# First mixer reordered by direction, its head outputs and gate rows moved beside other work, and weight splitting moved from GpSimd to ScalarE and VectorE

## The chip, the cores and the metric
The kernel runs on one core of a Trainium2 chip. The metric is device time in microseconds of one execution; three runs before the change took 2997.96, 3000.23 and 3006.75 us (median 3000.23).

## What is computed
Two transformer layers on 512 tokens of width 1024 (three kinds of attention, then a gated feed-forward network each), then one block with two recurrent mixers over 256 context and 512 latent tokens, then a last feed-forward network and norm. The change lies in the recurrent block. In fp32, cut to what matters:

```python
u, u_c = modulate(rms_norm(x)), modulate(rms_norm(ctx))      # latent and context tokens
p = split_cols(u @ w_in)      # first mixer: q, k, v, gate, low rank; second: q, k, v, gate; 16 gate rows; branches
# first mixer (gated linear attention), 4 heads of 128 keys x 256 values, both directions
log_a = log_sigmoid(low_rank @ w_up + b_dec) / 16            # one decay per token and key
b = cumsum(log_a within a chunk of 64)
scores = mask((q * exp(b)) @ (k * exp(-b)).T)
o = scores @ v + (q * exp(b)) @ S ;  S = exp(b_last) * S + (k * exp(b_last - b)).T @ v
y_gla = rms_norm(o, per head) * silu(gate)
# second mixer (mLSTM), 4 heads on the tokens in column order, both directions
f = log_sigmoid(gate rows f), i = gate rows i                # 4 rows x 4 heads of 768 tokens
m = running max of (m + f, i); rows of weights from f, i, m; convolution and silu on q and k
h = scan with those weights;  y_m = rms_norm(h) * sigmoid(gate)
x = x + g1 * ((sigmoid(b0) * (y_gla @ w0) + sigmoid(b1) * (y_m @ w1)) @ w_out)
```

## The kernel before, in words
Each engine has a program of its own, written out by hand as one Python function per engine; they meet at semaphores only, and each engine takes its queue in order. A `Program` counts what it has waited for; a `Banks` ring hands out PSUM banks: `fill` on TensorE waits until the bank's last content has been read, `take` on the reader waits until it is full. In this block ScalarE reads the ring `ab` (three banks: projections, transposed keys, decay inputs) and VectorE the ring `db` (two banks: scores, states, outputs). The `job`s of one ring must be taken in the order in which TensorE fills them.

*Projections.* A product of fp32 accuracy is three matmuls on high and low parts (`parts_steps`, 8 steps of 3 matmuls). The weights of the two mixers come as 24 pieces of 1 MB (`SECOND`: for each head `qk`, `v`, `gate`), loaded by SP alternately into two places (`PLACE`): piece j is loaded when piece j - 2 has been read for the last time. GpSimd waits for each landing and makes the high part (a cast) and the low part (a subtraction), `split_piece` (L762); TensorE waits for `piece_split`. GpSimd also brings the first four of eight tiles of the tokens into column order (`permute`, L597; VectorE does the other four) once all heads of the first mixer have been projected, and after that goes on with the pieces of the second mixer, the branches and the output.

*First mixer.* For each head, TensorE issues: decay inputs of direction 0, q of the next head, decay inputs of direction 1, k and two of the six v tiles of the next head, then `gla_scan` (L1263) for direction 0 and for direction 1, the rest of the next head's projections between them, then gate 1 and `head_outputs` (L1294: eight transposes). A scan is: scores, six key transposes, eleven state products (some projection steps between them), four outputs. ScalarE makes the decays (`decay_exponents`, L1868): two evacuations with the bias, abs, exp, ln, then, when VectorE has made the chunk sums, three exponents and one more. VectorE (`decays`, L2307) makes min, subtraction, scan, differences, and the decayed q, k (two forms). The tiles W1 to W5 are shared by both directions, so one direction's decays follow the other's. Then VectorE masks the scores, updates the states, adds the outputs (`gla_outputs`, L2338) and in `head_outputs` (L2350) scales by the root that ScalarE's `head_norm` (L1892) gives.

*Gate rows.* After the fourth head: 16 gate rows are projected, picked apart by four small products into 4 heads x 4 rows (`GR`), ScalarE adds the bias and makes abs, exp, ln; then `rows` (L2388) on VectorE for both directions, with q and k of the second mixer's first two heads on TensorE beside them. The second mixer starts when both directions are done.

The lines that set the order of one head on TensorE before:

```python
                decay_inputs(h, 0)
                if h + 1 < NH2:
                    run(nxt("q"))
                decay_inputs(h, 1)
                ...
                gla_scan(h, 0, nxt)
                gla_scan(h, 1, nxt)
                run(nxt("gate", 1))
                head_outputs()
```

## Time and profile before
| | |
|---|---|
| profiled execution | 3005.11 us, span 3003.2 us |
| TensorE busy | 2759.6 us, 92% |
| VectorE / ScalarE / GpSimd busy | 1296.2 / 986.0 / 1001.6 us |
| mean granted clock of TensorE | 0.951 of full speed |
| chain that ended last | PE 73%, DVE 9%, ACT 8%, DMA 6%, issue 2% |

In the profile PE is TensorE's matmuls and PEld its weight loads, DVE is VectorE, ACT ScalarE, POOL GpSimd, SP the engine that issues loads. Stretches are given in microseconds from the start of the span. PEclk is the granted clock of TensorE as a share of 2.4 GHz. A busy TensorE at half clock does half the work, so busy time alone doesn't tell how much of a stretch could go.

### The profile page before, as it was taken

How to read it: one execution, taken by the hardware profiler on the slowest of the kernel's cores; microseconds unless marked ns; L12 is line 12 of the kernel's file. 1: busy time of each engine (PE TensorE's matmuls, PEld its weight loads, DVE VectorE, ACT ScalarE, POOL GpSimd, SP SyncE). 2: the span in 40 equal slices, each digit the busy share in tenths (PEclk: the TensorE clock that was granted, in tenths of full speed). 3: DMA queues.
4: the chain of work that ended last, by engine and by line, in shares of the span. 5: the costliest groups of instructions: out<-in, count | busy, mean ns of one | idle time of the engine just before them, and what ended most of it. 6: DMA issues, size and time to landing. Idle time of an engine off the chain costs nothing.

```text
span 3003.2 us, 35461 instructions
## 1 busy us (share of the span) xinstructions
PE 2759.6 (92%) x13958; PEld 2141.7 (71%) x13958; DVE 1296.2 (43%) x1755; ACT 986.0 (33%) x1652; POOL 1001.6 (33%) x683
## 2 busy tenths in 40 slices
PE   7988999999999799999998888596998999899997
PEld 6866658887797574888876666465876565688886
DVE  2758445443354863544333344526333212333322
ACT  5468422222344872222223344322222100222221
POOL 5565403436545660134562322411220223200000
PEclk9999999999999999999998999797998999899998
DMA  5230024554422002355452111011111331233322
GB/s 127 91 65 1 19 70 119 148 134 133 140 75 84 18 1 59 104 137 139 133 145 66 43 29 42 28 29 28 43 43 42 80 88 57 65 104 95 88 87 67
DMA packets 386053, 230.39 MB, mean 77 GB/s; under 512 B 9340, under 2 KB 382204, under 8 KB 385888
## 3 DMA queue, kind: packets, MB, share of 16 engines
q1 hardware_dynamic: 383408, 224.09, 27.1%
q0 software_dynamic: 1952, 1.94, 0.8%
q8 instruction: 111, 1.82, 0.3%
q10 hardware_dynamic: 528, 2.10, 0.2%
q14 instruction: 54, 0.44, 0.0%
HBM read 226.01 MB, written 2.10 MB: 76 GB/s over the span
## 4 chain that ended last, share of the span: by engine, by line
PE 73%; DVE 9%; ACT 8%; DMA 6%; issue 2%; POOL 0%; SPq 0%; DVEq 0%; ACTq 0%; POOLq 0%
PE ps L815 63%; PE scores L815 7%; DMA raws<-in_w_down 5%; PE ps L957 1%; ACT wH L1770 1%; DVE R L2058 1%; DVE R L2316 1%; ACT R L1895 0%; DVE spare L2068 0%; ACT U L1609 0%; DMA ring<-in_w_in 0%; DVE R L2314 0%; DVE QK_parts L2048 0%; ACT spare L1632 0%; DVE R L2356 0%
## 5 line engine op out<-in xcount | busy, mean ns | idle before, releaser
L815 PE MATMUL ps<-xH,wH 128*128 128x512 f32 x1000 | 396.9, 397 | 8.3 <-DVE xL L2227 8.3
L815 PE MATMUL ps<-xL,wH 128*128 128x512 f32 x1000 | 391.3, 391 | 0.0
L815 PE MATMUL ps<-xH,wL 128*128 128x512 f32 x1000 | 390.9, 391 | 0.0
L1770 ACT ACTIVATE wH<-raws 128x2048 fp32r<-128x2048 f32 (+1 forms) x114 | 192.9, 1692 | 503.8 <-PE ps L815 307.3
L2253 DVE TENSOR_TENSOR wL<-raws,wH 128x2048 fp32r<-128x2048 f32 (+1 forms) x113 | 233.7, 2068 | 286.4 <-ACT wH L1770 286.3
L815 PE MATMUL ps<-ring_parts,U_parts 128*128 128x256 f32 (+1 forms) x1936 | 311.7, 290 | 12.8 <-DVE ring_parts L2110 6.2
L716 POOL TENSOR_TENSOR spare<-spare,cvec 128x1024 f32<-128x1024 f32 x64 | 124.5, 1946 | 563.6 <-DMA spare<-in_w_ada 563.6
L815 PE MATMUL ps<-R 128*64 128x128 f32 (+6 forms) x1768 | 276.6, 344 | 29.3 <-DVE R L2334 4.6
L815 PEld LDWEIGHTS ps<-ring_parts,U_parts 128*128 128x128 f32 x1936 | 277.7, 197 | 25.9 <-issue 22.6
L815 PEld LDWEIGHTS ps<-R 128*64 128x64 f32 (+2 forms) x1768 | 171.3, 166 | 131.1 <-issue 77.0
L768 POOL CAST ring_parts<-ring 128x2048 fp32r<-128x2048 f32 x28 | 54.6, 1951 | 547.5 <-DMA ring<-in_w_in 540.5
L815 PE MATMUL ps<-U_parts,ring_parts 128*128 128x512 f32 (+2 forms) x720 | 217.1, 392 | 18.3 <-ACT R L1863 18.3
L815 PEld LDWEIGHTS ps<-xH,wH 128*128 128x128 f32 x1000 | 188.7, 189 | 52.9 <-issue 8.5
L815 PE MATMUL ps<-R,ring 128*128 128x512 f32 x496 | 217.5, 596 | 1.3 <-DVEq L56 1.3
L815 PEld LDWEIGHTS ps<-xH,wL 128*128 128x128 f32 x1000 | 188.9, 189 | 39.8
L815 PEld LDWEIGHTS ps<-xL,wH 128*128 128x128 f32 x1000 | 189.0, 189 | 38.4 <-issue 1.0
L815 PE MATMUL ps<-hH,wH 128*128 128x512 f32 x528 | 210.6, 399 | 1.1 <-DVE wL L2253 1.1
L815 PE MATMUL ps<-hL,wH 128*128 128x512 f32 x528 | 207.5, 393 | 0.0
L815 PE MATMUL ps<-hH,wL 128*128 128x512 f32 x528 | 207.0, 392 | 0.0
L718 POOL TENSOR_TENSOR spare<-spare 128x512 f32<-128x512 f32 (+2 forms) x192 | 199.4, 1038 | 15.1
L815 PEld LDWEIGHTS ps<-R,ring 128*128 128x128 f32 x496 | 94.4, 191 | 113.9 <-issue 111.2
L815 PEld LDWEIGHTS ps<-U_parts,ring_parts 128*128 128x128 f32 (+1 forms) x720 | 134.1, 192 | 56.5 <-issue 28.2
(408 smaller groups left out, 4697.5 us busy)
## 6 DMA issues: line engine op xcount, KB each, us to landing
raws<-in_w_gate_up SPq DMA_DIRECT2D x88, 512.0 KB, 5.5
ring<-in_w_in SPq DMA_DIRECT2D x34, 1024.0 KB, 5.9
spare<-in_w_ada SPq DMA_DIRECT2D x64, 512.0 KB, 4.1
raws<-in_w_down SPq DMA_DIRECT2D x32, 704.0 KB, 6.1
raws<-in_w_ffn_in SPq DMA_DIRECT2D x44, 512.0 KB, 5.1
ring<-in_w_in SPq DMA_DIRECT2D x22, 512.0 KB, 6.0
raws<-in_w_ffn_out SPq DMA_DIRECT2D x16, 704.0 KB, 4.5
ring<-in_w_o SPq DMA_DIRECT2D x6, 896.0 KB, 5.4
```

The lines of the kernel that those rows point to most:

```text
L716: pg.do(nc.gpsimd.tensor_tensor(w_, w_, bc(cvec[:, :, ADA[a][1]], P, 2), ALU.mult))
L718: pg.do(nc.gpsimd.tensor_tensor(w[:, 0:n_ * P], w[:, 0:n_ * P], w[:, n_ * P:2 * n_ * P], ALU.add), ada_summed if n_ == 1 else None)
L768: pg.do(nc.gpsimd.tensor_copy(high, raw_))
L815: return nc.tensor.matmul(o, a, b, start=first, stop=last)
L957: ins = nc.tensor.transpose(bank[:, s_ * P:(s_ + 1) * P], PX[a % 4][:, c, s_ * P:(s_ + 1) * P], ident[:, :])
L1770: ap.do(f(wH[:, g % 2, 0:n], raws[:, g % 2, 0:n], ACT.Copy), wh_ready)
L2058: vp.do(v.tensor_reduce(nmax[:, n:n + 2], SP[a % 2][:, :, :], AX.X, ALU.max, negate=True), s_max)
L2253: vp.do(v.tensor_tensor(wL[:, g % 2, 0:n], raws[:, g % 2, 0:n], wH[:, g % 2, 0:n].bitcast(F32), ALU.subtract), wl_ready)
L2316: vp.do(v.tensor_tensor_scan(W3[:, r], seg[:, :], W1[:, r], 0.0, ALU.mult, ALU.add), b_ready)
```

## The change
Seven edits, all in the recurrent block.

1. `gla_scan` takes the whole order of a head. Direction 0: scores, key transposes, decay inputs of direction 1, `head_outputs` of the head before, q of the next head, states with k 1 between them, k 0, v 0 to v 2, outputs. Direction 1: scores, key transposes, decay inputs of the next head's direction 0, v 3, states with v 4 and v 5, gates 0 and 1, outputs. For the last head: v of the second mixer's first head before, beside and after the states of direction 0, the 16 gate rows and its gate in direction 1.
2. ScalarE's `decay_exponents` is cut into `decay_logs` and `decay_exponents`; VectorE's `decays` into `decay_sums` (min and subtraction in one instruction) and `decayed`. They are put during the scan ahead of theirs.
3. `gla_outputs` is cut into `masked`, `states` and `gla_outputs`; VectorE makes the next decays before it adds the outputs.
4. ScalarE makes the high part of pieces 1 to 23 (`second_part`), VectorE the low part (`second_low`). GpSimd keeps piece 0, the two small ones, and those of branches and output.
5. GpSimd permutes five tiles, VectorE three.
6. Gate rows: the bias is added and the logarithm made on 16 rows, while TensorE makes the gate of the second mixer's first head; then both are picked apart.
7. `head_outputs` of the last head goes behind the second mixer's first q and k, on VectorE between `rows(0)` and the convolution.

```diff
@@ TensorE, gla_scan
                 key_transposes(kd[:, d, :])
                 transposed = ab.n
-                run(nxt("v", (2, 5)[d]))
+                if d == 0:
+                    decay_inputs(h, 1)
+                    if h > 0:
+                        head_outputs()
+                    run(nxt("v", 0) if last_head else nxt("q"))
+                    beside_states = nxt("v", 1) if last_head else nxt("k", 1)
+                elif last_head:
+                    pe.wait_ge(gates_split, 1)
+                    parts_job(ab, lambda b: b[0:16, 0:256], small(GATES_AT, 16), XcP)
+                    parts_job(ab, lambda b: b[0:16, :], small(GATES_AT, 16), XP)
+                    beside_states = nxt("gate", 0)
+                else:
+                    decay_inputs(h + 1, 0)
+                    run(nxt("v", 3))
+                    beside_states = chain(nxt("v", 4), nxt("v", 5))
                 pe.wait_ge(a_free, transposed)
...
                     if order.index(c) % 2:
-                        some(between, 2)
-                if d == 0:
-                    run(nxt("v", 4))
+                        some(beside_states, 2)
+                run(beside_states)
+                if d == 0 and last_head:
+                    pp.more(u_permuted, 2)
+                    for m in range(2, 6):
+                        run(nxt("v", m))
+                elif d == 0:
+                    run(nxt("k", 0))
+                    for m in range(3):
+                        run(nxt("v", m))
+                elif last_head:
+                    run(nxt("gate", 1))
+                    pe.wait_ge(gates_logged, 1)
...
+                else:
+                    run(nxt("gate", 0))
+                    run(nxt("gate", 1))
                 pp.more(sc_ready)
                 pp.more(st_ready)
@@ ScalarE
+            def second_part(name, h):
...
+                act.wait_ge(piece_in[i], landed[i])
+                raw_, high, _ = place_parts(i)
+                ap.do(f(high, raw_, ACT.Copy), second_high)
...
             for h in range(NH2):
                 n_ = h + 1
-                decay_exponents(h, 0, [("q", 0)] if n_ < NH2 else ())
-                decay_exponents(h, 1, [("k", 0)] if n_ < NH2 else ())
+                if h > 0:
+                    head_norm(gla_squares)
+                keys_by_token(kdt)
+                decay_logs(h, 1)
+                second_part("v", n_)
                 if n_ < NH2:
-                    evacuate(n_, ("k", 1))
-                evacuate(n_, ("v", 0), ("v", 1))
+                    evacuate(n_, ("q", 0), ("k", 1), ("k", 0))
+                    decay_exponents(h, 1)
+                    evacuate(n_, ("v", 0), ("v", 1), ("v", 2))
...
                 keys_by_token(kdt)
+                if n_ < NH2:
+                    decay_logs(n_, 0)
+                    second_part("gate", n_)
+                    evacuate(n_, ("v", 3), ("v", 4), ("v", 5))
+                    decay_exponents(n_, 0)
+                    evacuate(n_, ("gate", 0), ("gate", 1))
+                    if n_ + 1 < NH2:
+                        second_part("qk", n_ + 1)
...
                 head_norm(mlstm_squares)
                 beside(("gate", 1))
+                if h + 2 < NH2:
+                    second_part("qk", NH2 + h + 2)
@@ VectorE
+            def second_low(name, h):
...
+                dve.wait_ge(second_high, j)
+                vp.do(v.tensor_tensor(low, raw_, high.bitcast(F32), ALU.subtract), piece_split)
...
+                vp.more(dec_ready)
+                masked(0)
+                if h > 0:
+                    head_outputs(h - 1, 3, Y)
+                second_low("v", h + 1)
                 if h == NH2 - 1:
+                    dve.wait_ge(head_in, NH2)
                     for k in range(POOL_TILES, KT):
                         permute(vp, v, k, og_row)
                     vp.also(u_permuted)
...
+                states(gla_order(0), ST, DV, lambda c: dec[:, 0, c:c + 1])
+                decay_sums(h, 1)
+                decayed(h, 1)
+                if h == NH2 - 1:
+                    second_low("gate", NH2)
+                gla_outputs(0)
+                vp.more(dec_ready)
+                masked(1)
+                states(gla_order(1), ST, DV, lambda c: dec[:, 1, c:c + 1])
+                if h + 1 < NH2:
+                    second_low("gate", h + 1)
+                    decay_sums(h + 1, 0)
+                    decayed(h + 1, 0)
+                    if h + 2 < NH2:
+                        second_low("qk", h + 2)
...
+                gla_outputs(1)
+                vp.also(og_ready)
...
             rows(0)
+            head_outputs(NH2 - 1, 3, Y)
+            second_low("qk", NH2 + 1)
...
             convolve(0)
             rows(1)
+            second_low("v", NH2 + 1)
```

In the prologue TensorE makes k 0, the decay inputs of head 0, then the six v and the two gates; ScalarE makes both halves of head 0's first decays between k 0 and the evacuations of v.

## Rows read from the trace of the kernel before

**Rows 1.** Windows: length, busy (instructions) of PE, PEld, DVE, ACT, POOL, PEclk, DMA.
```profile
1741.10:1824.20 83.10, 71.64 (x402) 53.23 (x401) 35.62 (x54) 31.93 (x51) 19.30 (x6) 0.94 0.14 39
```

**Rows 2.** Waits of TensorE, 1602 to 2069: total us, times, longest.
```profile
PE scores L815 <- DVEq L56: 29.9, 1, 29.9
PE ps L1352 <- ACT R L1943: 22.2, 1, 22.2
PE ps L815 <- ACT R L1863: 18.3, 2, 9.6
PE scores L815 <- ACT R L1863: 8.3, 1, 8.3
...
PE ps L815 <- DVE R L2334: 4.6, 8, 0.6
PE ps L815 <- DVEq L56: 3.0, 4, 0.7
PE ps L1299 <- DVEq L56: 2.5, 4, 0.7
```

**Rows 3.** Chain of waits inside the second long idle: start, us, what.
```profile
1747.75 0.94 ACT R L1877
1748.80 4.16 DVE R L2314
1752.98 1.77 DVE R L2316
```

**Rows 4.** Timeline of VectorE, the first head's decays: start, us, what.
```profile
1665.63 5.93 DVE L2316 TENSOR_TENSOR_SCAN R<-C,R 128x768 f32<-128x768 f32 x1
1671.60 0.96 DVE L2319 TENSOR_TENSOR R<-R 128x768 f32<-128x768 f32 x1
```

**Rows 5.** Windows: the nine stretches of busy TensorE at half clock.
```profile
1602.81:1608.75 5.94, 5.94 (x14) 2.42 (x15) 5.62 (x10) 5.28 (x9) 0.00 (x0) 0.50 0.01 3
...
1895.47:1898.88 3.41, 3.41 (x12) 1.30 (x8) 0.84 (x2) 0.00 (x0) 0.18 (x1) 0.50 0.00 0
...
sum 38.82, PE 38.35 PEld 28.74 DVE 16.23 ACT 21.55 POOL 0.18; mean PE 4.26 PEld 3.19 DVE 1.80 ACT 2.39 POOL 0.02
```

**Rows 6.** Chain of waits: one v projection, and four outputs of a scan.
```profile
1627.98 2.88 PE scores L815 x24
...
1811.89 4.91 PE ps L815 x24
```

**Rows 7.** Timeline of VectorE: two state updates with two projection steps between pairs.
```profile
1724.62 1.00 DVE L2334 SCALAR_TENSOR_TENSOR R<-R,dec,ps 128x256 f32<-128x256 f32 x2 [1.23 <-PE ps L815]
```

**Rows 8.** Groups by form: copies and subtractions of a weight piece on three engines.
```profile
L1770 ACT ACTIVATE wH<-raws 128x2048 fp32r<-128x2048 f32 x66 | 126.6, 1917 | 207.8 <-PE ps L815 207.4 <-ACT rt L1597 0.2
...
L2253 DVE TENSOR_TENSOR wL<-raws,wH 128x2048 fp32r<-128x2048 f32 x21 | 48.1, 2292 | 25.3 <-ACT wH L1770 25.3
...
L769 POOL TENSOR_TENSOR ring_parts<-ring,ring_parts 128x2048 fp32r<-128x2048 f32 x28 | 129.4, 4621 | 2.2
```

**Rows 9.** Timeline of VectorE: its wait for the head norm.
```profile
1738.19 0.18 DVE L2354 RECIPROCAL rsg<-rsg 128x4 f32<-128x4 f32 x1 [3.93 <-ACT rsg L1896]
```

**Rows 10.** Timeline of VectorE: the first of the rows of direction 0.
```profile
2030.20 1.75 DVE L2391 TENSOR_TENSOR_SCAN R<-C,R 4x768 f32<-4x768 f32 x1
```

**Rows 11.** Windows: idles of TensorE and the granted clock after them.
```profile
770.03:772.07 2.04, 0.00 (x1) 0.00 (x1) 2.00 (x2) 0.00 (x0) 1.91 (x2) 1.00 0.34 83
772.49:775.90 3.41, 3.41 (x9) 2.66 (x9) 0.49 (x1) 0.00 (x0) 1.24 (x1) 0.50 1.03 280
...
1752.11:1762.35 10.24, 3.92 (x18) 3.95 (x19) 5.90 (x6) 6.18 (x9) 0.03 (x1) 0.50 0.01 2
...
2138.30:2148.50 10.20, 10.20 (x60) 9.07 (x61) 1.50 (x2) 4.20 (x6) 5.14 (x2) 1.00 0.34 99
```

**Rows 12.** Timelines of ScalarE and TensorE at the second mixer's first head's end.
```profile
2138.15 0.60 ACT L1854 ACTIVATE R<-ps 128x512 f32<-128x512 f32 x1
...
2138.30 1.10 PE L1299 MATMUL ps<-ident,R 128*128 128x128 f32 x8 [1.55 <-DVEq L56]
```

More of the change, by code:

```diff
@@ L779, in _ @@
             split_small(lr_in, LR_AT, 2 * RANK, lr_split)
-            for j in range(1, 4):
-                split_piece(j)
             split_small(gates_in, GATES_AT, 16, gates_split)
-            for j in range(4, SECOND.index(("gate", NH2))):
-                split_piece(j)
             pool.wait_ge(head_in, NH2)
@@ L788, in _ @@
             pg.also(u_permuted)
-            for j in range(SECOND.index(("gate", NH2)), len(SECOND)):
+            landed = [16 * sum(len(second_dmas(j)) for j in range(N_PROJ) if PLACE[j] == i) for i in range(4)]
+            for j in range(N_PROJ, len(SECOND)):
                 split_piece(j)
@@ L1307, in _ @@
             pe.wait_ge(tab_in, 80)
-            for name, m in PROJECTIONS[2:]:
+            ranked = ab.n
+            run(first("k", 0))
+            pe.wait_ge(a_free, ranked)
+            decay_inputs(0, 0)
+            for name, m in PROJECTIONS[3:]:
                 run(first(name, m))
-            pe.wait_ge(a_free, ab.n)
             for h in range(NH2):
                 nxt = projections(h + 1)
-                decay_inputs(h, 0)
-                if h + 1 < NH2:
-                    run(nxt("q"))
-                decay_inputs(h, 1)
-                if h + 1 < NH2:
-                    run(nxt("k", 0))
-                    run(nxt("k", 1))
-                else:
-                    pp.more(u_permuted, 2)
-                run(nxt("v", 0))
-                run(nxt("v", 1))
                 gla_scan(h, 0, nxt)
                 gla_scan(h, 1, nxt)
-                run(nxt("gate", 1))
-                head_outputs()
-            pe.wait_ge(gates_split, 1)
-            parts_job(ab, lambda b: b[0:16, 0:256], small(GATES_AT, 16), XcP)
-            parts_job(ab, lambda b: b[0:16, :], small(GATES_AT, 16), XP)
-            gates_out = ab.n
             run(nxt("q"))
-            pe.wait_ge(a_free, gates_out)
-            for g in range(4):
-                job(ab, lambda b: b[0:NH2, 0:256], [(ident[0:16, 4 * g:4 * g + 4], G16[:, 0:256])])
-                job(ab, lambda b: b[0:NH2, :], [(ident[0:16, 4 * g:4 * g + 4], G16[:, 256:768])])
             run(nxt("k", 0))
             run(nxt("k", 1))
+            head_outputs()
             nxt = projections(NH2 + 1)
@@ new lines, in _ @@
+                keys_by_token(kdt)
+                if n_ < NH2:
+                    decay_logs(n_, 0)
+                    second_part("gate", n_)
+                    evacuate(n_, ("v", 3), ("v", 4), ("v", 5))
[3 more added lines that the diff above has]
+                        second_part("qk", n_ + 1)
+            for a, n in ((0, 256), (256, 512)):
+                bank = ab.take(act)
+                ap.do(f(G16[:, a:a + n], bank[0:16, 0:n], ACT.Identity, bias=bgate[:, 0:1]), a_free)
@@ L1923, in _ @@
+            ap.do(f(LF16, G16, ACT.Abs))
+            ap.do(f(LF16, LF16, ACT.Exp, scale=-1.0))
+            ap.do(f(LF16, LF16, ACT.Ln, bias=ones[0:16, 0:1]), gr_ln)
+            evacuate(NH2, ("gate", 0))
+            second_part("qk", NH2)
+            evacuate(NH2, ("gate", 1))
             for g in range(4):
@@ L1925, in _ @@
                     bank = ab.take(act)
-                    ap.do(f(GR[:, g, a:a + n], bank[0:NH2, 0:n], ACT.Identity, bias=bgate[:, g:g + 1]), a_free)
-            ap.do(f(LT, GR[:, 1:4:2, :], ACT.Abs), gr_abs)
-            ap.do(f(LT, LT, ACT.Exp, scale=-1.0))
-            ap.do(f(LT, LT, ACT.Ln, bias=ones[0:NH2, 0:1]), gr_ln)
+                    copy_out(GR[:, g, a:a + n], bank[0:NH2, 0:n], a_free)
+            ap.also(gr_ready)
+            head_norm(gla_squares)
+            evacuate(NH2, ("q", 0))
+            second_part("qk", NH2 + 1)
             def activate(h):
@@ L1961, in _ @@
                     beside(("v", (1, 4)[d]))
+                    if d == 1 and follows:
+                        second_part("gate", NH2 + h + 1)
                     ap.more(wexp_in)
@@ L2351, in head_outputs @@
                 g_ = head(h)[3]
-                vp.also(og_ready)
                 vp.more(og_root)
@@ L2373, in _ @@
                     vp.also(u_permuted)
[L2374 to L2378 removed]
+                states(gla_order(0), ST, DV, lambda c: dec[:, 0, c:c + 1])
[13 more added lines that the diff above has]
+                        second_low("qk", h + 2)
+                else:
+                    vp.more(gr_ln)
+                    vp.do(v.scalar_tensor_tensor(LF16, G16, 0.0, LF16, ALU.min, ALU.subtract), gates_logged)
+                    second_low("qk", NH2)
+                gla_outputs(1)
+                vp.also(og_ready)
             vp.do(v.memset(seg[:, :], 1.0))
             vp.do(v.memset(seg[:, 0:SEQ2:P], 0.0))
[L2383 to L2386 removed]
+            vp.more(gr_ready)
             def rows(d):
@@ L2458, in mlstm_outputs @@
                 vp.do(v.tensor_tensor(SCm, Wm, KQ, ALU.mult), sc_ready)
+                if d == 1 and h + 1 < NH2:
+                    second_low("gate", NH2 + h + 1)
                 states(mlstm_order(d), STm, DV + 1, lambda c: dec[:, d, c:c + 1])
@@ L2475, in _ @@
                     mlstm_outputs(h, d)
+                vp.also(og_ready)
                 head_outputs(h, 4, YM)
+                if h + 2 < NH2:
+                    second_low("qk", NH2 + h + 2)
             for m in range(KT):
```

105 lines of the change are left out of this document (59 added, 46 removed).

## The prediction
> **What bounds the kernel now.** The windows view comes first. The first mixer and the gate rows after it fill 1602.8 to 2068.5 us of the span; a middle head takes 83.1 us, in which TensorE is busy 71.6 [rows 1]. The waits of TensorE there say where the rest is: 78.7 us in five long idles (29.9 + 22.2 + 18.3 + 8.3) and 10.1 us in short ones (4.6 + 3.0 + 2.5) [rows 2]. The chain of waits shows what is inside a long idle: decay inputs, then six ScalarE pieces (the last stands in the rows; the first began at 1742.71, and two are table loads of 1.28), then VectorE's subtraction and scan, then ScalarE again [rows 3]. It stands exposed because the next projection's bank is freed by a ScalarE evacuation queued behind the exponents. The subtraction took 4.16 us and one scan 5.93 us, while GpSimd's weight subtraction ran; a clean scan took 1.77 [rows 3, 4]. Last the clock: in nine stretches TensorE was busy for 38.35 us at half clock (1.2 GHz instead of 2.4), nearly all after these idles [rows 5]. At full clock half of that goes.
>
> **What is removed.** In the new order the decays of direction 1 are computed under k0 and v0 to v2 of the next head, those of the next head's direction 0 under gates 0 and 1. From the end S of direction 0's states: VectorE's last update 0.5, sum 1.04 (no such 768-wide form in the trace: between the plain two-input one of 768, 0.96 [rows 4], and 1.44, three state updates of 256 columns at 0.48; I take 1.04, near the plain one), scan 1.8, so S + 3.4; on ScalarE a table load 1.28 and exponents of 0.65, 0.65, 0.25 and 0.85 to S + 7.2, VectorE's first two products beside them, its last 0.96: ready at S + 8.2. TensorE needs them after k0, three v (2.9 each) and four outputs (4.9) [rows 6], at S + 16.8. From the end T of direction 1's states the same, 2.3 later for a weight piece, is ready at T + 10.4, and needed after the rest of v5 (2.2), two gates (5.6 each) and the outputs, at T + 18.9. Both chains are hidden with 8 us to spare; without that cover each is worth one long idle of 8 to 10 us. The idle of 29.9 us held four permuted tiles on VectorE between the two decays of the last head; three remain, GpSimd takes five and starts earlier. The idle of 22.2 us was the row arithmetic after all projections; now head_outputs of the last head and q, k0, k1 of two heads lie beside it. All five idles go: 78.7. Of the short ones, the wait for the eleventh state in direction 0 stays (4 x 0.6), 7.7 goes. Of the half clock all but the first 5.9 us (before anything changed) goes: 32.4 / 2 = 16.2. Sum removed: 102.6.
>
> **What is added.** The weight pieces are split by ScalarE (a 128x2048 copy 1.92 us) and VectorE (subtraction 2.29) instead of GpSimd (a cast first, then a subtraction of 4.62) [rows 8]; 23 pieces, so 4.2 us of latency each, now inside the queues that free TensorE's banks. I go through one head, times from the end E of the outputs before.
> - *Head norm ahead of key copies* (heads 1 to 3). og_ready to the root takes 3.9 us [rows 9] at the head of ScalarE's queue; the copies of the transposed keys and both decay evacuations wait behind it. TensorE does scores, transposes and one decay job (2.4), then needs a bank that comes free at E + 5.0, and og_normed at E + 6.2: 2.9 us each, 8.7.
> - *v piece ahead of the states* (heads 0 to 2). decay_logs 6.2, copy 1.92, subtraction 2.29: the first state update is free to run at E + 16.9. TensorE gets through head outputs (1.1), q (5.6, twice the columns of a v), two state jobs and two steps of k1 at 2.2 us a pair (start to start of two rows like the one shown) [rows 7] by E + 15.1: 1.8 each, 5.4.
> - *gate piece after the states* (heads 0 to 2): 0.5 + 2.3 against 2.2 of v5 left: 0.6 each, 1.8.
> - *Next qk piece between decays and outputs* (heads 0 and 1). It waits for gate 1's evacuation at T + 14.7; copy and subtraction end at T + 18.9. The outputs start at T + 14.0 with two banks, the third waits: 2.9 each, 5.8. Its DMA, issued on SP once v5 is read, lands some 8 us after T, 6 us early.
> - *Prologue.* Three banks hold v0 to v2 while ScalarE does the decays of head 0 (12.8 us from the decay inputs, against 8.9 of projections): 4.2; then the piece of head 1's q: 1.5.
> - *Last head.* Its first projection v0, which TensorE reaches at E + 7.3, needs the v piece behind decay_logs, at E + 16.5: 9.2; the states wait for three permuted tiles (6.6 us): 1.3; one bank 0.5.
> - *Rows.* VectorE's rows take 8 to 10 us a direction (the first direction's began at 2030.2 [rows 10] and ended at 2040.1). The second mixer's next q waits for a piece whose subtraction (2.3) stands on VectorE behind the last head's two gated products (2 x 1.2) and starts only after the transposes on TensorE: 4.7. From there VectorE has the convolution (5.6 and small ones 0.8) and rows of direction 1 (8.6), ScalarE then a table load and four exponents (3.9): 18.9 us, against 14.3 of q, k0 and k1 on TensorE: 4.6.
>
> These waits sum to 47.7. Nine of them are over 2 us. An idle of 2.04 us was followed by 3.41 us at half clock, worth 1.7; an idle of 1.55 left the clock whole [rows 11, 12]; one of 8.67 brought 10.24 us at half. New waits are nearest to the first: 9 x 1.7 = 15.3. Gain in the mixer: 102.6 - 63.0 = 39.6.
>
> The Trainium skill (TensorE: Matmul & The Clock Gate, "HAM oscillation — how this bites in real kernels") speaks against trading a few long idles for many short ones: matmuls in bursts with waits between them can lose the clock again at every burst. [...]
>
> **Second mixer.** There GpSimd's splits were done early. Now the qk piece waits for head norm and gate 1's evacuation, which ended at 2138.75; copy to 2140.7, subtraction to 2143.1, where TensorE went on to this q at the end of the transposes, 2139.4 [rows 12]: 3.7 us, plus 1.7 of clock, for two heads: 10.8. Its v piece has 8.5 us of k0 and k1 beside its 4.2, and its gate piece runs where VectorE has passed the scores on and waits for the first state; both I cost at nothing. If that cover failed, each of these five would cost up to 4.2.
>
> Sum: 39.6 - 10.8 = 28.8 us. The profiled execution took 3005.1 us (span 3003.2), 4.9 above the median of the three runs, 3000.2. So 2976 on the profiled one, and 2971 against the median.
>
> **Rivals.**
> 1. *The short waits leave the clock whole.* For it: several idles of about 1.5 us did. Against: 2.04 did not. Eleven times 1.7 comes back: 28.8 + 18.7 = 47.5, 2953 us. Chance 0.20.
> 2. *The last head and the rows only move their wait.* Three tiles on VectorE, GpSimd beside it on the others, where the scan stretched beside GpSimd from 1.77 to 5.93 [rows 3, 4], and the row chain of both directions still end last. I count 30.5 us of gain there (idles 29.9 + 22.2 and clock 8.4, from four of the nine stretches, less 30 of new waits and clock). Without it: 1.7 slower, 3002 us, no change. This is also the case in which the change does not overlap the gate rows as it says. Chance 0.14.
> 3. *The clock oscillates.* Each of eleven waits brings 10.24 us at half clock, 5.1 instead of 1.7: 37.4 more, 3009 us. For it: the fp32 outputs, scores and transposes round these waits twice fell to half clock (one stands in the rows) with short idles only. Against: they fell for 3.41 us [rows 5]. Chance 0.12.
> 4. *The weight parts land on the path.* ScalarE and VectorE take their queues in order, so any piece that is late holds evacuations and state updates behind it, and with them TensorE's three and two banks. Of 23 x 4.2 = 96.6 us I have 36 exposed; all of it exposed adds 61: 3032 us, slower. It decides from seven more fully exposed pieces (28.8 / 4.2). Against: ScalarE is busy 32 of a head's 83 us and VectorE 36 [rows 1], and each gains only some 6. Chance 0.08.
>
> My own forecast keeps 0.46, with a range of 2955 to 2988. The whole range reaches from below rival 1 to the slower cases but the fourth: 2942 to 3006, which leaves out about 0.17. About 0.3% (9 us) can be told from no change: faster than 2991 takes 0.43 of my own case, all of rival 1 and 0.07 of the second; within it lie 0.03 of mine, 0.06 of the second and 0.10 of the third; slower has the fourth, 0.02 of the third and 0.01 of the second. So 0.70, 0.19, 0.11.
>
> **What would show it.** Right: no idle of TensorE over 6 us from the first decay to the second mixer, except one of about 9 us before the last head's v0; waits of 2 to 3 us before head outputs and inside the outputs of heads 0 and 1; the scan at 1.77 everywhere; q of the second mixer's third and fourth heads 4 us late; first v of the second mixer's scan some 40 us earlier than 2068.5. Wrong, if the 29.9 us idle returns before the states of the last head, if the half clock covers more than 40 us of busy TensorE in the first mixer, or if ScalarE's weight copies wait for DMA.

## The result: 2972.6 us, and where the profile after shows it

The changed kernel took 2972.55 us (median of four runs, 2971.57 to 2979.16), the kernel before 2999.1 beside it (2993.36 to 3006.75): ratio 0.9915, 95% interval 0.9888 to 0.9941. The forecast was 2971. The profiled execution took 2971.57 us, with a span of 2969.8 and a mean granted clock of 0.958 (before 0.951).

The windows view cut at the same two pieces of work gives the account. The columns are as in [rows 1]; the first row of each kernel runs from the first projection to the first transposes of the row maxima, the second from there to the first matmuls of the last FFN. Before:

```profile
1602.81:2067.03 464.22, 373.76 (x2049) 278.46 (x2049) 204.77 (x293) 166.63 (x257) 123.64 (x50) 0.89 0.14 37
2067.03:2608.44 541.41, 504.61 (x2091) 367.98 (x2092) 153.61 (x329) 84.16 (x147) 129.53 (x43) 0.91 0.20 56
```

After:

```profile
1592.55:2024.65 432.10, 386.40 (x2048) 282.16 (x2048) 205.12 (x295) 189.53 (x269) 17.55 (x22) 0.92 0.15 39
2024.65:2574.81 550.16, 505.75 (x2091) 368.35 (x2092) 169.14 (x336) 97.46 (x154) 89.83 (x31) 0.91 0.20 55
```

The first mixer with the gate rows lost 32.1 us, the second (with the branch gates behind it) gained 8.75, and the last stage stayed within 0.2. The first mixer began 10.3 us earlier. Of these, 4.5 us lie in the norm ahead of the projections, where the change took GpSimd's work away. The other 5.8 lie ahead of that, where nothing was changed: the end of the previous FFN stands anywhere from 1571.9 to 1582.1 us in the traces of this study. So the change itself is worth 4.5 + 32.1 - 8.75 = 28 us by the trace.

In the first mixer TensorE was idle 90.5 us before (464.22 - 373.76) and 45.7 after. But it was busy 12.6 us longer, with the same instructions: the half clock did not go with the idles. The waits of TensorE after, 1620 to 2030 us (total, times, longest), against [rows 2]:

```profile
PE ps L812 <- DVE ring_parts L2365: 12.8, 4, 6.9
PE ps L812 <- ACT R L1620: 10.9, 5, 3.9
PE ps L812 <- DVE R L2407: 6.8, 2, 3.4
PE ps L1363 <- ACT R L1988: 4.8, 1, 4.8
PE ps L812 <- DVE R L2392: 3.2, 5, 0.6
PE scores L812 <- ACT R L1620: 2.5, 1, 2.5
PE ps L1330 <- DVEq L56: 1.5, 1, 1.5
```

L2365 is the low part of a weight piece (6.9 ahead of the last head's v0, 4.4 ahead of the second mixer's second q), L1620 an evacuation by ScalarE (3.9 in the prologue, 2.1 to 2.7 in front of three head outputs), L2407 the outputs of heads 0 and 1, L1988 the second direction's exponents. No idle of 29.9, 22.2 or 9 is left; the longest is 6.9. The clock, in two of its stretches at half (the last head, and the outputs of head 1):

```profile
1899.73:1916.83 17.10, 8.69 (x34) 6.77 (x32) 12.34 (x17) 8.31 (x9) 8.33 (x10) 0.50 0.00 1
...
1814.40:1817.81 3.41, 3.41 (x12) 1.32 (x9) 0.75 (x2) 0.00 (x0) 0.00 (x0) 0.50 0.00 0
```

TensorE was busy at half clock for 53.8 us of the first mixer, against 37.4 before. A second trace of the same kernel has 44.6 there, and the same 432 us. The groups of the stage show the split (ScalarE's high parts, VectorE's low parts) and the scan, all at the durations of [rows 8] and of the clean scan [rows 3]; 0.8 us is all the idle time ahead of ScalarE's copies, so they did not wait for DMA:

```profile
L1888 ACT ACTIVATE ring_parts<-ring 128x2048 fp32r<-128x2048 f32 x16 | 30.6, 1914 | 0.8
```

```profile
L2365 DVE TENSOR_TENSOR ring_parts<-ring,ring_parts 128x2048 fp32r<-128x2048 f32 x16 | 36.7, 2292 | 67.5 <-ACT ring_parts L1888 66.9
L2371 DVE TENSOR_TENSOR_SCAN R<-C,R 128x768 f32<-128x768 f32 x8 | 14.1, 1758 | 0.3
```

In the second mixer TensorE's waits, 2055 to 2275 us, have the two new ones for q, in its second and third heads' scans:

```profile
PE ps L812 <- DVE ring_parts L2365: 3.7, 1, 3.7
PE scores L812 <- DVE ring_parts L2365: 3.7, 1, 3.7
```

And the gain that was not forecast: the timelines of GpSimd and VectorE in the norm ahead of the projections (start, us, what). Before, with GpSimd's cast and subtraction of the second piece at 1591.60 to 1598.48:

```profile
1591.60 1.97 POOL L768 CAST ring_parts<-ring 128x2048 fp32r<-128x2048 f32 x1
1593.65 4.83 POOL L769 TENSOR_TENSOR ring_parts<-ring,ring_parts 128x2048 fp32r<-128x2048 f32 x1
```

```profile
1591.85 2.26 DVE L2227 TENSOR_TENSOR ring_parts<-R,U_parts 128x512 fp32r<-128x512 f32 x1
1594.15 0.75 DVE L2231 SCALAR_TENSOR_TENSOR R<-xT,gm,ps 128x512 f32<-128x512 f32 x1
1594.93 3.83 DVE L2234 TENSOR_SCALAR R<-R,mod 128x512 f32<-128x512 f32 x1
```

After, without it:

```profile
1586.25 0.69 DVE L2281 TENSOR_TENSOR ring_parts<-R,U_parts 128x512 fp32r<-128x512 f32 x1
1586.98 0.75 DVE L2285 SCALAR_TENSOR_TENSOR R<-xT,gm,ps 128x512 f32<-128x512 f32 x1
1587.76 0.49 DVE L2288 TENSOR_SCALAR R<-R,mod 128x512 f32<-128x512 f32 x1
```

### The profile page after: what moved, and what is told of

Its sections match the earlier page's. It is cut to its first block, busy times and chain, and to the rows that moved or that the text cites. A ratio compares the mean times of both kernels' runs of the same rounds, so it can differ in the third digit from the quotient of the medians.

```text
span 2969.8 us, 35461 instructions
## 1 busy us (share of the span) xinstructions
PE 2772.8 (93%) x13958; PEld 2146.7 (72%) x13958; DVE 1306.4 (44%) x1765; ACT 1021.7 (34%) x1671; POOL 849.5 (29%) x641
## 4 chain that ended last, share of the span: by engine, by line
PE 75%; ACT 9%; DVE 7%; DMA 6%; issue 2%; POOL 0%; SPq 0%; ACTq 0%; DVEq 0%; POOLq 0%
PE ps L812 65%; PE scores L812 8%; DMA raws<-in_w_down 5%; ACT wH L1781 1%; PE ps L954 1%; DVE R L2112 1%; DVE ring_parts L2365 1%; ACT ring_parts L1888 1%; ACT spare L1643 1%; ACT R L1648 0%; ACT U L1620 0%; DVE R L2285 0%; DMA ring<-in_w_in 0%; DVE R L2288 0%; ACT R L1620 0%
## 5 line engine op out<-in xcount | busy, mean ns | idle before, releaser
L812 PE MATMUL ps<-ring_parts,U_parts 128*128 128x256 f32 (+1 forms) x1952 | 319.7, 293 | 23.9 <-DVE ring_parts L2365 7.4
L812 PE MATMUL ps<-R 128*64 128x128 f32 (+6 forms) x1768 | 283.2, 349 | 32.6 <-DVE R L2407 6.8
L812 PEld LDWEIGHTS ps<-ring_parts,U_parts 128*128 128x128 f32 x1952 | 284.8, 200 | 39.3 <-issue 28.0
L679 POOL TENSOR_TENSOR ring_parts<-ring,ring_parts 128x2048 fp32r<-128x2048 f32 (+2 forms) x23 | 99.7, 4339 | 123.4 <-ACT ring_parts L1568 123.1
```

What stands on the lines that cost most here:

```text
L679: pg.do(nc.gpsimd.tensor_tensor(low, slot(i, KT, n_), high.bitcast(F32), ALU.subtract), piece_low)
L812: return nc.tensor.matmul(o, a, b, start=first, stop=last)
```

## The experiments

Each stands against the kernel before by its ratio, and against the changed kernel by the difference of ratios (0.0010 is 3 us). A trace is one execution. "First mixer" and "second mixer" are the stretches of the two windows above. Each run has the kernel before beside it; the first four share one chip, the next four another, the next three a third, and the last ran apart.

**The changed kernel again** (after_again).

> The changed kernel as it stands, beside the next three, so that they are compared with it on the same chip. Both theories expect 0.9915 of the kernel before, within 0.003, and the same waits in the trace: 2.1 to 2.7 us ahead of three head outputs, 3.4 inside the outputs of heads 0 and 1, 6.9 ahead of the last head's v0, 4.4 and 4.8 at the rows, 3.7 twice in the second mixer.

Ratio 0.9922 (0.9908 to 0.9937), 2975.73 us; first mixer 431.6, second 550.1, all waits as expected. Both traces of the changed kernel thus agree on the length of every stage, and differ in the start and, in the first mixer, in what fills it: 386.4 us of busy TensorE and 45.7 idle in the first, 382.1 and 49.5 here.

**GpSimd splits the v piece of head 0** (v0_on_gpsimd).

```diff
 split_small(lr_in, LR_AT, 2 * RANK, lr_split)
+split_piece(1)
...
-second_part("v", 0)      # ScalarE
-second_low("v", 0)       # VectorE
```

> GpSimd splits the v piece of head 0 as in the kernel before, early, while VectorE makes the last FFN's sums into normed parts. Theory: the changed kernel starts its projections 16.5 us after the end of that FFN instead of 20.9 because GpSimd's split of this piece no longer stretches VectorE's operations there (2.26 and 3.83 us against 0.69 and 0.49). Then the 20.9 come back and about 0.5 us ahead of k0 goes: 4 us slower than the changed kernel, 0.1%. Rival: the earlier start came from somewhere else (run to run): 16.5 stay, and the time is the same or 0.5 lower.

Ratio 0.9962 (0.9950 to 0.9974): 12 us slower than the changed kernel, three times the forecast. The theory held in its place. From the FFN's end to the projections it took 22.2 us instead of 17.5, and VectorE's two stretched operations are back to the digit, so the stretch comes from GpSimd's split:

```profile
1583.19 2.26 DVE L2282 TENSOR_TENSOR ring_parts<-R,U_parts 128x512 fp32r<-128x512 f32 x1
...
1586.27 3.83 DVE L2289 TENSOR_SCALAR R<-R,mod 128x512 f32<-128x512 f32 x1
```

The rest came where nothing was edited. The first mixer took 434.1 us, 2.5 more, and the second 561.8 instead of 550.1, with the same idle time (44.6 and 44.4 us) and 109.8 us of busy TensorE at half clock instead of 85.6; half of the 24.2 more is 12.1. That asked for an experiment of its own, the last one below.

**The qk piece behind the outputs** (qk_after_outputs).

```diff
-                    if h + 2 < NH2:
-                        second_low("qk", h + 2)
...
                 gla_outputs(1)
                 vp.also(og_ready)
+                if h + 2 < NH2:
+                    second_low("qk", h + 2)
```

> VectorE makes the low part of the next qk piece behind the outputs of direction 1 and not ahead of them (heads 0 and 1). Theory: the two waits of 3.4 us inside these outputs go, and with each some 1.7 us of half clock: 10 us faster than the changed kernel. Rival 1, the clock takes no notice of such waits: 6.8 faster, the stretches at half clock stay. Rival 2, the wait only moves: the 2.3 us of the low part now delay the masked scores and the first state of the next head, and the gain is 2 us or less.

Ratio 0.9884 (0.9864 to 0.9904): 11 us faster than the changed kernel. The direction-1 scans of heads 0 and 1, in the windows view of the changed kernel (after_again):

```profile
1700.11:1739.29 39.18, 35.04 (x186) 24.91 (x185) 18.25 (x24) 17.13 (x21) 0.00 (x0) 0.96 0.20 54
1781.93:1821.04 39.11, 34.95 (x186) 24.84 (x184) 18.24 (x24) 17.13 (x21) 0.00 (x0) 0.96 0.21 54
```

and with the move:

```profile
1693.48:1727.78 34.30, 33.57 (x187) 24.57 (x185) 15.96 (x23) 17.13 (x21) 0.00 (x0) 1.00 0.22 56
1770.44:1804.74 34.30, 33.57 (x187) 24.56 (x185) 15.96 (x23) 17.12 (x21) 0.00 (x0) 1.00 0.22 59
```

Each loses 4.8 to 4.9 us: 3.4 of idle and 1.4 of busy time, as the clock is whole now. So a wait of 3.4 does cost about 1.5 of clock here, and the wait did not move. In this trace too the second mixer took more, 557.0 us.

**The head norm behind q** (norm_behind_q).

```diff
 keys_by_token(kdt)
+if 0 < h and n_ < NH2:
+    head_norm(gla_squares)      # was ahead of the key copies
...
 run(nxt("q"))
+head_outputs()                  # heads 1 and 2; was ahead of q
```

> For heads 1 and 2 (not the last), ScalarE copies the transposed keys ahead of the head norm, and TensorE runs the next q ahead of the head outputs' transposes. Theory: the waits of 2.1 and 2.5 us ahead of the head outputs go, since q (5.6 us) covers the norm (3.9 us): with 1.7 us of half clock each 8 us faster than the changed kernel. Rival 1: the clock stays as it is, 4.7 faster. Rival 2: the products of the head outputs on VectorE now end later, the v piece's low part and the first state update with them, and TensorE waits there instead: no faster, with waits of 2 us or more ahead of the third state.

Ratio 0.9937 (0.9922 to 0.9953): no faster, if anything 4 us slower; first mixer 438.6 instead of 431.6. Rival 2 it is. TensorE's waits in heads 1 and 2 now end with the first state update (L2394), which stands on VectorE behind the head outputs' products (L2426) and the low part of the v piece:

```profile
PE ps L812 <- DVE R L2394: 7.0, 2, 3.5
...
PE ps L812 <- DVE R L2426: 2.6, 4, 0.9
```

**The new order, with GpSimd splitting** (split_on_gpsimd). All calls of second_part and second_low do nothing; GpSimd splits pieces 1 to 12 ahead of the permutation and the rest behind it, as before.

> The new order of the work, but GpSimd splits all weight pieces as in the kernel before (the split by ScalarE and VectorE undone). Theory: the order makes the gain. The long idles stay away, since the decay chains have 8 us to spare and a scan beside GpSimd takes about 4 us longer and a subtraction 3; the waits for late pieces (3.4 twice, 6.9, 4.4, 3.7 twice, 25 us with some 10 of clock) go, and the stretched VectorE operations and 4.4 us in the norm before the projections eat part of that: 2955 to 2975, not slower than the changed kernel. Rival: the split by VectorE makes the gain, since GpSimd's subtraction beside VectorE holds the scans and the states: above 2985, with waits of 4 us and more ahead of scores and outputs.

Ratio 0.9872 (0.9856 to 0.9887), 2967.76 us: 13 to 15 us faster than the changed kernel, as the theory had it. So of the two halves of the change the order makes all of the gain, and the split by ScalarE and VectorE on the whole costs time. Not everywhere, though. Heads 0 to 2 are mostly faster (head 0: 69.4 us against 81.7), and the second mixer takes 536.9 us. But the norm loses its 4.7 us, and TensorE waits 9.7 us in the prologue, 10.8 for the last head's states and 18.0 for the rows:

```profile
PE ps L1367 <- ACT R L1987: 18.0, 1, 18.0
PE ps L816 <- ACT R L1624: 15.1, 3, 9.7
PE ps L816 <- DVE R L2386: 10.8, 1, 10.8
```

The scan took 2.28 us in the mean of eight there, against 1.76 in the changed kernel. VectorE's timeline shows what GpSimd has to do with the three waits. Ahead of them stand a scan of the prologue, a cast of the last head's permuted tiles and a product of the rows, each beside a subtraction of GpSimd's (1633.37 to 1638.48, 1909.02 to 1913.74, 2019.84 to 2024.39); in the changed kernel they take 1.76, 0.43 and 0.94 us:

```profile
1634.13 5.96 DVE L2367 TENSOR_TENSOR_SCAN R<-C,R 128x768 f32<-128x768 f32 x1
...
1909.42 4.61 DVE L601 CAST U_parts<-R 128x512 fp32r<-128x512 f32 x1
...
2020.07 5.13 DVE L2488 TENSOR_TENSOR R<-R,mrow 4x768 f32<-4x768 f32 x1
```

In the rows, convolution and second direction took VectorE 26.0 us instead of 14.5, which is most of the 13.2 that this wait grew. So the order alone does not clear the gate rows: with the split off GpSimd there, the wait is 4.8 us in the changed kernel and 6.8 in middle_on_gpsimd.

**The decays of direction 1 late** (decays_late). In heads 0 to 2:

```diff
 run(nxt("k", 0))
 for m in range(3):
     run(nxt("v", m))
+decay_inputs(h, 1)              # was ahead of the head outputs
...
+gla_outputs(0)                  # VectorE
 decay_sums(h, 1)
 decayed(h, 1)
-gla_outputs(0)
```

> In heads 0 to 2 the decays of direction 1 are made after v2 of the next head and after the outputs of direction 0 are under way, not during the scan of direction 0 (one half of the new order undone; the last head and direction 0 stay). Theory: each of three long idles returns: from the decay inputs 6.2 us to the logarithm, 2.8 for sum and scan, 4.4 to the last product, less 4.9 of outputs, 8 to 10 us each, and 3 to 5 us of half clock behind each: 33 to 45 us slower than the changed kernel. Rival: the queues of ScalarE and VectorE, not the place of the decays, set the time of a head (TensorE would wait as long elsewhere): under 15 us slower.

Ratio 1.0047 (1.0032 to 1.0063), 39 us slower than the changed kernel. Three idles of 9.0 us are back ahead of the scores of direction 1:

```profile
PE ps L812 <- DVE R L2387: 26.9, 3, 9.0
```

The first mixer took 471.3 us, 39.7 more; 27 of it are these waits, the rest mostly half clock (71.1 us busy instead of 44.6). This one half of the new order is worth more than the whole gain.

**The second mixer's qk pieces early** (second_qk_early).

```diff
+second_part("qk", NH2 + h + 2)  # ScalarE
 head_norm(mlstm_squares)
 beside(("gate", 1))
-second_part("qk", NH2 + h + 2)
...
 vp.also(og_ready)
+second_low("qk", NH2 + h + 2)   # VectorE
 head_outputs(h, 4, YM)
-second_low("qk", NH2 + h + 2)
```

> In the second mixer ScalarE copies the next qk piece ahead of the head norm, and VectorE makes its low part while ScalarE takes the head norm's squares (heads 0 and 1 of it). Theory: the two waits of 3.7 us ahead of q go, with 1.7 us of half clock or more each: 11 us faster than the changed kernel. Rival 1: the clock is unchanged, 7.4 faster. Rival 2: the copy stands ahead of the gate's evacuation or waits for its DMA, and the head norm comes later: less than 3 us faster.

Ratio 0.9853 (0.9830 to 0.9876): 19 to 21 us faster than the changed kernel by the ratio, 13 by the stage in the trace, where both waits of 3.7 are gone:

```profile
2026.66:2564.00 537.34, 499.71 (x2091) 363.77 (x2092) 169.41 (x336) 97.49 (x154) 89.84 (x31) 0.92 0.21 56
```

TensorE is idle 6.8 us less than in after_again and busy 6.0 less. Rival 1, a clock that takes no notice (7.4), is out by the ratio.

**Last head, rows, prologue** (last_and_rows).

```diff
+if n_ == NH2:
+    second_part("v", n_)        # ahead of decay_logs(h, 1)
...
+second_part("qk", NH2 + 1)
 head_norm(gla_squares)
 evacuate(NH2, ("q", 0))
-second_part("qk", NH2 + 1)
...
+second_low("qk", NH2 + 1)       # VectorE
 vp.more(gr_ready)
 rows(0)
 head_outputs(NH2 - 1, 3, Y)
-second_low("qk", NH2 + 1)
...
 decay_logs(0, 0)
+evacuate(0, ("v", 0))
 decay_exponents(0, 0)
```

> Three small moves: the last head's v piece is copied ahead of its decay logarithms; the qk piece of the second mixer's second head is split ahead of the row arithmetic; in the prologue v0 is evacuated between the logarithm and the exponents. Theory: the wait of 6.9 us ahead of the last head's v0 falls to 2 or 3 (bound by head norm and head outputs), that of 4.4 goes, but the wait for the second direction's exponents grows by some 2, and the 3.9 us of the prologue fall to 2: 8 to 10 us faster than the changed kernel with the clock. Rival: the row chain on VectorE sets the end of this stage whatever lies ahead of it (the first two gains turn into a longer wait for the exponents): 3 us or less.

The first mixer took 422.8 us, 8.8 less, as expected: prologue, last head's first scan, and second scan with rows, in this order:

```profile
1594.13:1650.69 56.56, 55.04 (x317) 45.03 (x318) 22.02 (x26) 27.58 (x39) 0.75 (x2) 0.95 0.15 39
1891.61:1939.63 48.02, 36.10 (x219) 27.59 (x217) 31.91 (x43) 20.70 (x32) 15.63 (x16) 0.86 0.08 21
1939.63:2016.88 77.25, 69.86 (x327) 45.27 (x325) 42.70 (x72) 35.25 (x51) 0.00 (x0) 0.91 0.17 43
```

against 60.8, 49.6 and 80.8 in after_again. The wait ahead of v0 fell only to 4.3, with 1.7 at the first state behind it. The ratio, 0.9902 (0.9883 to 0.9921), tells little from the changed kernel: in this trace the second mixer took 559.0 us and gave it all back.

**The three moves together** (three_moves): qk_after_outputs, second_qk_early and last_and_rows.

> The moves of qk_after_outputs, second_qk_early and last_and_rows together. From their traces: the first mixer 432 us less 10 less 9, the second 550 less 13, so 32 us faster than the changed kernel, 2941. Rival: the two mixers are not independent. In four runs whose second mixer was unchanged it took 557 to 562 us instead of 550, with the same idle time and 15 to 25 us more of it at half clock; if a shifted start brings that again, 20 to 24 us faster and not 32.

Ratio 0.9816 (0.9792 to 0.9840): 30 us faster than the changed kernel. First mixer 408.7, second 547.4: part of the rival as well, with 95.1 us at half clock in the second, against 73.4 in second_qk_early.

**Permuted tiles between the state updates** (permutes_beside_states): three_moves, and in VectorE's states of the last head, after every second update, `permute(vp, v, *beside.pop(0))` for one of the six parts.

> As three_moves, and VectorE's three permuted tiles of the last head stand between its state updates (one part, two copies, 1.04 us, after every second update; two updates with their waits take 2.2 us, 0.96 of it busy) and not ahead of the first. Theory: in last_and_rows the wait ahead of the last head's v0 had only moved to its first state, behind these tiles (6.7 us and more); now it goes, with half clock behind it: 8 to 10 us faster than three_moves. Rival: the tiles lengthen every pair of updates, and the states wait as long in pieces: 3 us or less.

Ratio 0.9807 (0.9780 to 0.9835), no difference from three_moves. The wait at the first state went, but it had been 1.9 there, not 6.7; 2.1 now stand ahead of v2, for the last tile, and 4.3 ahead of v0 as before. The theory had put the 6.9 in the wrong place. In the traces the first mixer took 415.7 us here and 408.7 in three_moves, the second 535.7 and 547.4, each with the same idle time within 0.7: what differs is busy time at half clock (41.4 against 29.3 us, 69.3 against 95.1).

**GpSimd for the middle pieces** (middle_on_gpsimd). Pieces 3 to 12 are split by GpSimd, with its own count; the rest as in the changed kernel, with the moves that the expectation names.

```diff
+ON_POOL = range(3, 13)
...
+for j in ON_POOL[1:]:
+    split_piece(j)              # GpSimd, ahead of its permuted tiles
...
+if j in ON_POOL:
+    return                      # in second_part and second_low
```

> Pieces from the qk of head 1 to the v of the second mixer's first head are split by GpSimd again, which is idle there; the first two and all later ones stay with ScalarE and VectorE. With it the order of norm_behind_q, the moves second_qk_early and last_and_rows (its v piece is on GpSimd now) and the permuted tiles between the states. Theory: the v pieces are what made norm_behind_q fail (3.5 us ahead of the third state in heads 1 and 2) and what cost head 0 its 2.3 us; without them the scans of heads 1 and 2 lose some 6 us each (42.7 to 36), head 0's 5, the outputs' wait of 3.4 twice: 15 to 20 us faster than permutes_beside_states. Rival: GpSimd's subtraction beside VectorE stretches scans and updates enough to bring waits back, as in the last head of split_on_gpsimd (10.8 us): not faster.

Ratio 0.9747 (0.9721 to 0.9773), 2928.38 us: 18 us faster than permutes_beside_states, 50 faster than the changed kernel, 76 faster than the one before. Head 0, head 1, head 2 and the last head's first scan:

```profile
1655.59:1724.98 69.39, 68.75 (x393) 50.47 (x391) 26.94 (x43) 27.62 (x40) 22.79 (x9) 1.00 0.23 59
1724.98:1800.04 75.06, 72.57 (x403) 52.75 (x401) 32.56 (x51) 30.64 (x49) 19.36 (x6) 0.98 0.17 44
1800.04:1874.62 74.58, 72.24 (x403) 52.49 (x401) 32.40 (x51) 30.62 (x49) 22.44 (x10) 0.98 0.15 43
1874.62:1920.22 45.60, 37.45 (x218) 29.52 (x217) 27.84 (x42) 18.80 (x31) 14.10 (x17) 0.89 0.09 23
```

Heads 1 and 2 of the changed kernel:

```profile
1734.60:1817.30 82.70, 75.68 (x403) 54.59 (x401) 38.13 (x54) 36.34 (x52) 0.00 (x0) 0.93 0.14 39
1817.30:1894.29 76.99, 72.62 (x402) 53.14 (x400) 35.84 (x53) 34.44 (x51) 3.42 (x5) 0.97 0.14 41
```

In head 0 TensorE is idle 0.6 us of 69.4, at full clock. Here the order of norm_behind_q works: in heads 1 and 2 the wait of 3.5 us at the first state is gone, with the v piece off VectorE, and what stays is 1.3 us a head behind the products of the head outputs, as there.

**A start 1.3 us later** (late_by_1us).

```diff
+for _ in range(6 * d):
+    ap.do(f(ssg[:, :], ssg[:, :], ACT.Copy))
 ap.do(f(rM[d], rM[d], ACT.Exp, scale=-1.0), rows_exp)
```

> The changed kernel, with six copies of a 128x4 tile onto itself on ScalarE (about 0.22 us each, 1.3 together) ahead of the last exponents of the row arithmetic, for which TensorE waits in any case; nothing else differs. The second mixer's first half-clock stretch began 2.0 to 2.1 us before its first transposes in the traces that took 550 us for it, and 2.3 us, 3.7 us or about 0 before them in those that took 557 to 562. Theory: where the work stands against these stretches settles what the second mixer takes, so a start 1.3 us later costs 7 to 12 us there, 9 to 13 in all, against the changed kernel. Rival: the stretches follow the work (they begin a fixed time after an idle), and 1.3 us is all that is lost.

The second mixer, first in after_again, then here:

```profile
2028.40:2578.46 550.06, 505.68 (x2092) 368.16 (x2092) 168.87 (x336) 97.48 (x154) 89.83 (x31) 0.91 0.20 55
```

```profile
2032.93:2592.19 559.26, 514.71 (x2092) 376.85 (x2093) 169.24 (x336) 97.49 (x154) 89.87 (x31) 0.89 0.20 54
```

9.2 us more, of which 9.0 are busy TensorE with the same instructions: 105.3 us at half clock instead of 85.6. But the start was not moved by the edit alone. It stood 4.5 us later than in after_again, because the first mixer had lost 3.1 us ahead of the edit, with 56.7 us of busy TensorE at half clock against 44.6. Measured from the stretch at half clock that began last before it (2.13 us before in after_again, 3.40 here) it stood 1.3 us later. The stage lost what was forecast (7 to 12); the whole trace is 13.7 us longer (9 to 13 were forecast). The ratio, 0.9940 (0.9928 to 0.9953), is only 5 to 8 us above the changed kernel's, and with these intervals the rival's 1.3 is not excluded by it. So it is shown that the same work can take 9 us more at half clock alone. That its place against the clock's stretches settles which it is agrees with eight traces (about 550 us where a stretch began 2.0 to 2.1 us before the start, 557 to 562 elsewhere), but this run doesn't show it by itself; what sets the stretches is open.

## Why the prediction was right, and where it was not

**The idles.** That all five long ones go was right. For the three of 8 to 10 us the reason given is shown: decays_late puts one half of the order back and three idles of 9.0 us return, where the cover was priced at 8 to 10. For those of 29.9 and 22.2 us no run undoes their moves one by one; 10.8 and 18.0 us stood in their places when GpSimd split again (split_on_gpsimd). Removed were 86.4 us of idle time, 47.7 were to be added: 38.7 less. The two traces have 44.8 and 41.0 less. The first v of the second mixer's scan, forecast some 40 us earlier than 2068.5, began at 2026.2; that was luck, since 10.3 of these 42.3 us are the earlier start of the first mixer. That the last head and the rows would only move their wait (the second rival) did not happen.

**The added waits** came out one by one: head norm 2.9 (measured 2.1, 2.5, 2.7), output wait 2.9 (3.4), gate piece 0.6 (0.7), prologue 4.2 (3.9) and the piece behind it 1.5 (1.2), last head's v0 9.2 (6.9), its permuted tiles 1.3 (none and 0.3), its bank 0.5 (1.0), q of the second mixer's second head 4.7 (4.4), exponents 4.6 (4.8), the two q of the second mixer 3.7 (3.7 and 3.7). What failed is the v piece ahead of the states, 1.8 in each of three heads: only head 0 shows it (2.9 in one trace; in the other TensorE came later, at half clock). In heads 1 and 2 TensorE is held up by the head norm first and arrives when the state is ready; the two were counted twice. norm_behind_q showed it from the other side: without the first wait the second is 3.5.

**The clock** is the term that was mis-sized. I took 38.35 us at half clock down to 5.9 and added nine times 3.41: 36.6 in all. The two traces of the changed kernel have 53.8 and 44.6. So the mixer gained 32.1 instead of 39.6, and by the sign that I had named myself (over 40 us) this step was wrong.

What failed first is the reading of [rows 5], that nearly all of the half clock stood after the long idles. Of the 38.35 us, 13.7 (stretches of 3.41, 3.41 and 6.83) had no wait of over 0.8 us in the 15 us before them. The longest begins where TensorE picks the gate rows apart, in products over 16 rows. I had it gone, and it stands in both traces of the changed kernel too, with no wait over 0.7 us in the 10 us before it. Before, then after:

```profile
2018.35:2025.18 6.83, 6.83 (x26) 5.05 (x25) 0.95 (x1) 5.70 (x6) 0.00 (x0) 0.50 0.00 0
```

```profile
1974.82:1981.62 6.80, 6.80 (x17) 2.10 (x14) 0.84 (x2) 1.26 (x3) 0.00 (x0) 0.50 0.11 30
```

A second misreading is in the third rival's price. The 10.24 us behind the idle of 8.67 are the length of the stretch, part of it the idle itself; TensorE was busy for 3.92 us of it [rows 11], worth 2.0 and not 5.1.

The price of a wait alone was good: qk_after_outputs gave 1.4 to 1.5 for one of 3.4, where I had 1.7 [rows 11]. In the last head the waits of 2.7, 1.5 and 6.9 close together kept the clock at half for 17.1 us, but TensorE was busy for only 8.7 of them, where two times 3.41 were forecast. The other rivals on the clock do no better: by the first it would have stayed whole; by the third every wait brings 10.24, where those of over 2 us in heads 0 to 2 brought 3.41 in one trace and 3.4 or 6.8 in the other. One of 1.2 us in head 0 was followed by 6.8 at half in one trace and by none in the other. The Trainium skill (TensorE: Matmul & The Clock Gate, "HAM oscillation — how this bites in real kernels") says that bursts with waits between them can pay for the clock at each burst. The trace agrees in kind, and for waits shorter than those of the section's example: each wait of over 2 us in heads 0 to 2 is followed by a stretch at half, mostly of a third of the length that the third rival took. TensorE's busy time missed the forecast by 13.5 us in the first trace and 9.2 in the second. Half clock accounts for 8.6 of the first (17.2 us more than 36.6, halved) and 4.0 of the second; the other 5 of each I could not place.

**The second mixer** was forecast 10.8 slower and is 8.75 slower: its idle time grew by 7.6 us (7.4 were forecast), its busy time by 1.1 (3.4). But the waits are not all of it: the stage takes 550 or 557 to 562 us with them, and 536 to 547 without them (second_qk_early, three_moves, permutes_beside_states, middle_on_gpsimd). That both traces of the changed kernel had 550 was luck.

**The weight parts** I had priced as exposed in part, without asking what the other choice costs in the new order. split_on_gpsimd answers it: the order alone would have been worth 13 to 15 us more. The chains that GpSimd stretches had come off the path in heads 0 to 2, so that the stretched scan of [rows 4] no longer mattered there; in the prologue, the last head's states and the rows they are still on it. Hence middle_on_gpsimd, which gives GpSimd the pieces between, is the fastest.

**Compensation.** The 28 us of the trace agree with the 28.8 forecast partly because misses cancel, which is luck: the mixer 7.5 us short, the norm 4.5 us better by an effect that I had not counted, the second mixer 2 better. I had read the stretch beside GpSimd in the decays [rows 3, 4] and not looked for it in the stage ahead.

## What to carry to other kernels

Take what is late off the path first, and then ask again which engine should do the side work: an engine that stretched the critical chain may be the right one where that chain has cover, and an engine that frees banks makes the banks wait for any side work put into its queue. Price waits one by one from the queue in front of each, and before adding two waits of one engine in the same stretch ask whether the first absorbs the second, as the head norm's did here. And judge a change of a few us by its stage and its idle time: two edits here won 9 to 10 us in their stage and lost 7 to 9 in another that they do not touch, to the clock.

## What the runs showed of the hardware

- The second mixer, instruction for instruction the same, took 550 us in three traces and 557 to 562 in five (v0_on_gpsimd, qk_after_outputs, decays_late, last_and_rows, late_by_1us), with up to 24 us more at half clock and the same idle time. In the three a stretch at half clock began 2.0 to 2.1 us before its start, in the five elsewhere.
- Beside GpSimd's split, VectorE's operation with a scalar went from 0.49 to 3.83 us and its two-input subtraction from 0.69 to 2.26, while the form with one PSUM operand kept its 0.75. The stretched operations end as if they had waited for GpSimd's instruction to end and then run at their own length: the scalar one at 1598.76, with GpSimd's subtraction ending at 1598.48 (0.49 later would be 1598.97), and the prologue's scan in split_on_gpsimd at 1640.09, with GpSimd's ending at 1638.48 (1.76 later would be 1640.24). The Trainium skill (GPSIMD Engine Reference, "8. Key points") says that GpSimd shares its SBUF interfaces with VectorE and contends with instructions of two SBUF inputs or in a two-port mode. The rows agree as to which forms suffer: the one with two SBUF inputs does, the one with an input in PSUM does not; which mode the third ran in, no row tells.
